# RWKV-7 recurrence: turn by feature and affine step one period later, keys' start before the block inversion, tile loads in two parts

## The reference, cut to what matters

```python
kk = heads(k * k_k); kk = kk * rsqrt(max(sum(kk * kk), 1e-24))
k = k * (1.0 + (a - 1.0) * k_a)
decay = exp(-exp(w))
# per token, 16 heads of 64 x 64:
sk = state @ kk_t
state = state * w_t - sk (x) (kk_t * a_t) + v_t (x) k_t
y = state @ r_t
# then per head:
y = (y - mean) * rsqrt(var + GN_EPS) * ln_w + ln_b
bonus = sum(r * k * r_k) * v
y = (y + bonus) * g
```

## Time and profile before

| | |
|---|---|
| time, three executions | 3096.55, 3098.84, 3102.23 us; median 3098.84 |
| the profiled execution's own time | 3100.76 us |
| its span | 3098.8 us |
| busy over the span | PE 2688.0 us (87%), DVE 1655.4 (53%), POOL 1257.8 (41%), ACT 932.7 (30%) |
| recurrence | about 1626 to 2235 us |
| mean granted TensorE clock | 0.944 of full speed |

### The profile page before, as it was taken

One profiled execution on the slowest core, in us unless ns is written; L12 is line 12 of the kernel. 1 busy time (PEld: TensorE's weight loads), 2 busy tenths in 40 slices (PEclk: granted clock), 3 DMA queues, 4 the chain that ended last, 5 costly groups with the idle time before them and its releaser, 6 DMA issues. The chain is left out here.

```text
span 3098.8 us, 48344 instructions
## 1 busy us (share of the span) xinstructions
PE 2688.0 (87%) x20064; PEld 2195.1 (71%) x20064; DVE 1655.4 (53%) x2070; ACT 932.7 (30%) x1543; POOL 1257.8 (41%) x630
## 2 busy tenths in 40 slices
PE   1787898999999999899994777777569999999999
PEld 1565666888877788677773667666557888878887
DVE  6844545756536444669734666776314544434444
ACT  2434433222233222455542223222124222222221
POOL 2532244444454444443433234333136344444443
PEclk9889998999999999999996888888789999999999
DMA  6421233555523223375563333333243233323333
GB/s 233 165 73 35 89 121 113 170 168 170 170 84 106 89 88 103 95 171 154 144 157 89 90 84 86 81 88 76 47 112 89 95 95 95 102 89 95 102 96 122
DMA packets 313433, 343.31 MB, mean 111 GB/s; under 512 B 231041, under 2 KB 231169, under 8 KB 313217
## 3 DMA queue, kind: packets, MB, share of 16 engines
q1 hardware_dynamic: 313216, 340.23, 37.5%
HBM read 298.29 MB, written 40.89 MB: 109 GB/s over the span
## 5 line engine op out<-in xcount | busy, mean ns | idle before, releaser
L687 POOL TENSOR_TENSOR wl<-w,wh 128x1024 fp32r<-128x1024 f32 x368 | 907.4, 2472 | 1304.0 <-ACT wh L728 1303.9
L180 PE MATMUL ps<-hi,wh 128*128 128x512 f32 x2208 | 881.8, 399 | 56.6 <-POOL wl L687 42.9
L181 PE MATMUL ps<-lo,wh 128*128 128x512 f32 x2208 | 868.3, 393 | 0.0
L182 PE MATMUL ps<-hi,wl 128*128 128x512 f32 x2208 | 867.9, 393 | 0.0
L728 ACT ACTIVATE wh<-w 128x1024 fp32r<-128x1024 f32 x368 | 388.1, 1056 | 716.2 <-DMA w<-in_ffn_w_in 528.7
L180 PEld LDWEIGHTS ps<-hi,wh 128*128 128x128 f32 x2208 | 419.8, 190 | 159.5 <-POOL wl L687 43.1
L994 DVE SCALAR_TENSOR_TENSOR xt<-ps,mod,xt 128x512 f32<-128x512 f32 x384 | 286.5, 750 | 431.8 <-PE ps L182 431.5
L181 PEld LDWEIGHTS ps<-lo,wh 128*128 128x128 f32 x2208 | 419.8, 190 | 89.3 <-issue 3.5
L182 PEld LDWEIGHTS ps<-hi,wl 128*128 128x128 f32 x2208 | 419.3, 190 | 89.6
L999 DVE TENSOR_TENSOR act<-ps,silu 128x512 f32<-128x512 f32 x88 | 60.9, 692 | 456.3 <-PE ps L182 456.3
L180 PE MATMUL ps<-act_hi,wh 128*128 128x512 f32 x704 | 281.7, 400 | 17.3 <-DVE act_lo L1003 9.7
(11 more groups left out here) (219 smaller groups left out, 3403.9 us busy)
## 6 DMA issues: line engine op xcount, KB each, us to landing
w<-in_ffn_w_in SPq DMA_DIRECT2D x176, 512.0 KB, 3.7
piece<-in_ada_w SPq DMA_DIRECT2D x96, 512.0 KB, 4.7
w<-in_ffn_w_out SPq DMA_DIRECT2D x88, 512.0 KB, 3.7
w<-in_w_rkv SPq DMA_DIRECT2D x48, 512.0 KB, 4.1
scratch<-silu SPq DMA_DIRECT2D x48, 256.0 KB, 3.1
scratch<-act SPq DMA_DIRECT2D x48, 256.0 KB, 3.0
w<-in_wqk SPq DMA_DIRECT2D x20, 512.0 KB, 4.7
xt<-in_xT SPq DMA_DIRECT2D x4, 2048.0 KB, 10.3
```

The lines of the kernel that those rows point to most:

```text
L180: pe.matmul(out, w_hi(k), x_hi(k), start=first and k == 0, stop=False)
L181: pe.matmul(out, w_hi(k), x_lo(k), start=False, stop=False)
L182: ins = pe.matmul(out, w_lo(k), x_hi(k), start=False, stop=last and k == kc - 1)
L687: pool.tensor_tensor(wl[n % NW][:, :, :], wr[n % NW][:, :, :], wh[n % NW][:, :, :].bitcast(F32), ALU.subtract).then_inc(*wlo.up)
```

## The change

A sixth argument, zp = chunk c-2, is added to `period`, and c runs to 17. `by_feature` (PE), `affine` (DVE), `finish` (POOL) and `store_z` (SP) are called for zp, one period later, and earlier in the lists. `begin(w)` moves ahead of `invert`, `bonus_value` ahead of `scale`. PE's `norms` waits for the bonus value. ACT's `squares` goes ahead of the copy of the turned keys. The tile loads are split: k, a and the decay's sigmoid as soon as POOL has k2, lprev and b of the chunk before; r behind `blocks_out`. POOL's `keys` does lprev first, bias has two buffers, and in POOL's list `bonus_and_bias` comes first.

```diff
-    for c in range(-RING, NC + 1):
-        period(at(c + 3), at(c + 2), at(c + 1), at(c), at(c - 1))
+    for c in range(-RING, NC + 2):
+        period(at(c + 3), at(c + 2), at(c + 1), at(c), at(c - 1), at(c - 2))
 # SP
 def load_tiles(ch):
-    sp.wait_ge(*g["rk_done"].at(ch))
-    sp.wait_ge(*g["ar_done"].at(2 * ch))
+    sp.wait_ge(*g["k2_done"].at(ch))
+    sp.wait_ge(*g["lq_done"].at(ch))
+    sp.wait_ge(*g["b_done"].at(ch))
     settle(sp)
-    for n, x in ((0, rt), (1, kt_), (3, st_), (4, at_)):
+    for n, x in ((1, kt_), (4, at_), (3, st_)):
         sp.dma_start(x[:, :, :], scr[n, ...]).then_inc(*g["tiles_in"].up)
+def load_r(ch):
+    sp.wait_ge(*g["rk_done"].at(ch))
+    sp.wait_ge(*g["ar_done"].at(2 * ch))
+    settle(sp)
+    sp.dma_start(rt[:, :, :], scr[0, ...]).then_inc(*g["r_in"].up)
-def period(w, x, d, y, zz):
-    load_gate(y); blocks_out(x); load_tiles(w); blocks_in(x); blocks_back(d); load_values(w); store_z(zz)
+def period(w, x, d, y, zz, zp):
+    load_gate(zz); load_tiles(w); blocks_out(x); load_r(w); blocks_in(x); store_z(zp); blocks_back(d); load_values(w)
 # POOL
 def keys(ch):
+    pool.wait_ge(*g["l_done"].at(ch + 1))
+    pool.tensor_tensor(lprev[:, :, :], lcum[:, :, :], st_[:, :, :], ALU.subtract).then_inc(*g["lq_done"].up)
     pool.wait_ge(*g["t1_done"].at(ch + 1))
...
-    pool.wait_ge(*g["l_done"].at(ch + 1))
-    pool.tensor_tensor(lprev[:, :, :], lcum[:, :, :], st_[:, :, :], ALU.subtract).then_inc(*g["lq_done"].up)
 def bonus_terms(ch):
     pool.wait_ge(*g["k2_done"].at(ch + 1))
+    pool.wait_ge(*g["r_in"].at(ch + 1))
-    normed_keys(x), bonus_and_bias(zz), bonus_terms(x), finish(zz), keys(w)
+    bonus_and_bias(zz), normed_keys(x), bonus_terms(x), finish(zp), keys(w)
 # ACT
-    root(zz), token_out(x, 1), squares(w)
+    root(zz), squares(w), token_out(x, 1)
 # PE
 def norms(ch):
     pe.wait_ge(*g["sq_done_w"].at(ch + 1))
-    pe.wait_ge(*g["z1_done"].at(max(ch - 3, 0)))
+    pe.wait_ge(*g["bonus_done"].at(ch))
 def by_feature(ch):
     pe.wait_ge(*g["ybd_done"].at(ch + 1))
     pe.wait_ge(*g["bonus_done"].at(min(ch + 4, NC)))
+    pe.wait_ge(*g["mx_done"].at(min(ch + 5, NC)))
-    solve_x(zz), level_x(y, 0), level_t(y, 0), solve_u(zz), level_x(y, 1), outputs(zz), gram(x, 0), state_products(zz),
-    level_t(y, 1), by_token(x, 0), by_token(x, 1), bonus_sums(x), gram(x, 1), by_feature(zz), by_token(x, 2), norms(w)
+    solve_x(zz), by_feature(zp), level_x(y, 0), level_t(y, 0), solve_u(zz), level_x(y, 1), outputs(zz), gram(x, 0),
+    state_products(zz), level_t(y, 1), by_token(x, 0), by_token(x, 1), bonus_sums(x), gram(x, 1), by_token(x, 2), norms(w)
 # DVE
 def begin(ch):
-    dve.wait_ge(*g["tiles_in"].at(4 * ch + 4))
+    dve.wait_ge(*g["tiles_in"].at(3 * ch + 3))
     dve.wait_ge(*g["kb_done"].at(ch))
+    dve.wait_ge(*g["rk_done"].at(ch))
 def decayed(ch):
...
+    dve.wait_ge(*g["r_in"].at(ch + 1))
-    bounded(x), level(y, 0, ..), products_k(d), level(y, 1, ..), decayed(x), centre(zz), products_b(x), new_state(zz), decayed_keys(x),
-    invert(d), variance(zz), invert_last(d), scale(zz), bonus_value(x), begin(w), affine(zz), decay_sums(w)
+    bounded(x), affine(zp), level(y, 0, ..), products_k(d), level(y, 1, ..), decayed(x), centre(zz), products_b(x), new_state(zz),
+    decayed_keys(x), begin(w), invert(d), variance(zz), invert_last(d), bonus_value(x), scale(zz), decay_sums(w)
```

More of the change, by code:

```diff
@@ L94 @@
 wkv_ybd_done wkv_yf_done wkv_z1_done wkv_bias_done wkv_z_step wkv_zeros g_in0*16 g_in1*16
-wkv_chunk_used wkv_post_done wkv_sub_step wkv_sub_done n_out*16 nd_in*16 t_out*16 img_zero*16 t_in0*16 t_in1*16 z_stored*16 z_in0*16 z_in1*16 z_hi z_lo stored*16
+wkv_chunk_used wkv_post_done wkv_r_in*16 wkv_sub_step wkv_sub_done n_out*16 nd_in*16 t_out*16 img_zero*16 t_in0*16 t_in1*16 z_stored*16 z_in0*16 z_in1*16 z_hi z_lo stored*16
 w_in0*16 w_in1*16 w_in2*16 w_in3*16 whi wlo tile_done x_done silu_done act_mul act_hi act_done
@@ L1248, in wkv_phase @@
                 state, xst, ust = st("state"), st("x_st"), st("u_st")
-                yc, ysq, yn, z, bias = st("y_centred"), st("y_sq"), st("y_norm"), st("z"), st("bias")
+                yc, ysq, yn, z, bias = st("y_centred"), st("y_sq"), st("y_norm"), st("z"), [st(f"bias{b}") for b in range(2)]
                 mean, var = sb("mean", [P, PAIRS], c=c), sb("var", [P, PAIRS], c=c)
@@ L1258, in wkv_phase @@
                          "m_step yc_done ysq_done var_done yrt_done yrn_done ybd_done yf_done z1_done bias_done z_step "
-                         "zeros sub_step sub_done chunk_used post_done").split()
-                g = {n: sig("wkv_" + n, 16 if n in ("tiles_in", "v_in") else 1) for n in names}
+                         "zeros sub_step sub_done chunk_used post_done r_in").split()
+                g = {n: sig("wkv_" + n, 16 if n in ("tiles_in", "v_in", "r_in") else 1) for n in names}
                 g_in = [sig(f"g_in{b}", 16) for b in range(2)]
@@ L1321, in load_tiles @@
                         def load_tiles(ch):
+                            sp.wait_ge(*g["k2_done"].at(ch))
[3 more added lines that the diff above has]
+                            for n, x in ((1, kt_), (4, at_), (3, st_)):
+                                sp.dma_start(x[:, :, :], scr[n, bass.ds(ch, 1)].rearrange("c p a n -> (c p) a n")).then_inc(*g["tiles_in"].up)
+                        def load_r(ch):
                             sp.wait_ge(*g["rk_done"].at(ch))
@@ L1325, in load_tiles @@
                             settle(sp)
-                            for n, x in ((0, rt), (1, kt_), (3, st_), (4, at_)):
-                                sp.dma_start(x[:, :, :], scr[n, bass.ds(ch, 1)].rearrange("c p a n -> (c p) a n")).then_inc(*g["tiles_in"].up)
+                            sp.dma_start(rt[:, :, :], scr[0, bass.ds(ch, 1)].rearrange("c p a n -> (c p) a n")).then_inc(*g["r_in"].up)
                         def load_values(ch):
@@ L1375, in _ @@
                                     sp.dma_start(image(t_img[b, w], h), state[h * HEAD:(h + 1) * HEAD, :, :]).then_inc(*img_zero.up)
-                        def period(w, x, d, y, zz):
-                            if y is not None:
-                                load_gate(y)
+                        def period(w, x, d, y, zz, zp):
+                            if zz is not None:
+                                load_gate(zz)
+                            if w is not None:
+                                load_tiles(w)
                             if x is not None:
@@ L1382, in period @@
                             if w is not None:
-                                load_tiles(w)
+                                load_r(w)
                             if x is not None:
                                 blocks_in(x)
+                            if zp is not None:
+                                store_z(zp)
                             if d is not None:
@@ L1389, in period @@
                                 load_values(w)
-                            if zz is not None:
-                                store_z(zz)
                         periods(period)
@@ L1422, in bonus_and_bias @@
                             pool.wait_ge(*g["bonus_done"].at(ch + 1))
-                            pool.tensor_tensor(bias[:, :, :], bonus[ch % RING][:, :, :], column(V_LNB), ALU.add).then_inc(*g["bias_done"].up)
+                            pool.tensor_tensor(bias[ch % 2][:, :, :], bonus[ch % RING][:, :, :], column(V_LNB), ALU.add).then_inc(*g["bias_done"].up)
                         def finish(ch):
@@ L1427, in finish @@
                             pool.wait_ge(*g["bias_done"].at(ch + 1))
-                            pool.tensor_tensor(z[:, :, :], z[:, :, :], bias[:, :, :], ALU.add).then_inc(*g["z_step"].up)
+                            pool.tensor_tensor(z[:, :, :], z[:, :, :], bias[ch % 2][:, :, :], ALU.add).then_inc(*g["z_step"].up)
                             pool.wait_ge(*g["z_step"].at(ch + 1))
@@ L1431, in finish, with period @@
                             pool.tensor_tensor(z[:, :, :], z[:, :, :], gt[ch % 2][:, :, :], ALU.mult).then_inc(*g["post_done"].up)
-                        def period(w, x, d, y, zz):
-                            if x is not None:
-                                normed_keys(x)
+                        def period(w, x, d, y, zz, zp):
                             if zz is not None:
@@ L1438, in period @@
                             if x is not None:
-                                bonus_terms(x)
-                            if zz is not None:
-                                finish(zz)
+                                normed_keys(x), bonus_terms(x)
+                            if zp is not None:
+                                finish(zp)
                             if w is not None:
@@ L1527, in period @@
                                 root(zz)
+                            if w is not None:
+                                squares(w)
                             if x is not None:
```

(15 more changed lines are left out.)

## The result

| | before | after |
|---|---|---|
| time, median of 7 runs each | 3100.12 us | 3108.72 us (3103.58 to 3112.06) |
| ratio, 95% interval | | 1.0025 (1.0015 to 1.0034) |
| the profiled execution's own time, span | 3100.76, 3098.8 | 3104.75, 3102.8 |

The change made the kernel slower by 0.25%, 8.6 us in the medians. Forecast were 3096 us and, as the likeliest, no change that can be told. The time lies inside the whole range of 3082 to 3113 us, but above the forecast's own range of 3089 to 3103, and the change is clear of the noise in the direction to which 27 in 100 were given.

What follows compares the result with a forecast made beforehand. No engine is full; a chain through several engines, 0.9 us longer than a DRAM round trip, sets the period. Steady +0.7, head -1.2, drain -2.7 sum to -3.2 us: 3096 us from 3098.84; own range 3089 to 3103, whole 3082 to 3113.

Steps and rivals of the forecast that it cites:

- Part 1: Turn by feature and affine step one period later: the DRAM round trip then sets the first level product, -0.9 us a period.
- T to X: From T, DVE's copy of the inverted diagonal blocks, to X, PE's next first level product: 10.1 us a period.
- Part 2: Keys' start (kk and k) in DVE's run ahead of the inversion: +1.3 us a period; its loads in time, 0.
- X to T: DVE's long run from PE's first level product (X) to its copy of the inverted blocks (T): 24.05 us a period.
- Part 3: POOL through before DVE's two decayed-key steps, which save 1.8 us; gram product then held by the outputs: -1.5 us.
- Part 4: SP's reordered waits, stores and tile loads, and the doubled bias: 0 us.
- Part 5: PE's new idle stretch ahead of the first level product lowers its clock, giving 24.05 us from X to T.
- Rival B: Clock lost for most of X to the outputs: period 35.7 us, 3114 us in all, slower; chance 0.22.
- steady sum: Twelve steady periods of the recurrence: 34.15 us a period against 34.09, +0.7 us over the twelve.
- Head: First passes of the recurrence: -5.1 us from earlier loads and key steps, +3.9 in the next three periods, -1.2 us.
- Drain: End of the recurrence: last chunk's right side starts ahead of the turn by feature, -2.7 us.
- Outside the recurrence: Time before and after the recurrence: no term in the sum, so no change.

Runs made afterwards that it cites:

- e_back_late: As e_begin_back, with POOL's two last steps of z also waiting for b_dec: 3073.57 us, ratio 0.9917 to the kernel before.
- e_pe_fill: Changed kernel plus five unread constant products on PE between the turn by feature and the first level's products: 3090.74 us, ratio 0.997 to the kernel before.
- e_begin_back: Changed kernel with the keys' start (two DVE steps) moved back behind the bonus value: 3077.57 us, ratio 0.9928 to the kernel before.

## Why the prediction was wrong

Its mechanism was right, and its sum was too low, on the wrong side of nothing. Point by point, with the means of the profiles of either kernel:

- *Part 1, X set by the DRAM round trip.* Right: the norms' product at T + 1.11, X 0.09 us behind the landing in every period. The size was off. The prediction took 10.1 us for T to X; it was 10.3, 10.5 and 10.4 in the three profiles, 0.3 more. The landing itself came at T + 10.2 to 10.4, where the two profiles of before give 10.2 and 9.9, and the 0.09 us from landing to start was left out.
- *Part 2, the keys' start, +1.3.* Right: X to T is 22.84 us with it (the clock up, POOL out of the way) and 21.5 without it, in e_back_late.
- *Part 3, POOL's order, -1.5.* Right: the two steps took 1.50 and 1.53 us in the mean before and 0.75 and 0.68 after, 0.78 and 0.75 in the second profile:

```profile
L1713 DVE TENSOR_TENSOR ar<-r,e_pos 128x512 f32<-128x512 f32 x12 | 9.0, 752 | 3.7 <-ACT e_neg L1471 3.7
L1716 DVE SCALAR_TENSOR_TENSOR ar<-kk,e_prev 128x512 f32<-128x512 f32 x12 | 8.2, 684 | 0.0
```

- *Part 4, SP and the loads, 0.* Right: in the period shown k's load is issued at T + 10.5, and DVE comes to kk at T + 26.6 (1982.47) without a wait.
- *Part 5, the clock.* It fell as the row of before had shown. Of 33 periods (eleven in each profile after) six were at 1.00 behind X, with 22.8 to 23.5 us from X to T; 21 had 2.8 to 3.4 us at 0.50 and took 23.8 to 24.4; six had 5.1 to 5.9 us and took 24.9 to 25.2. The mean is 24.2 against the 24.05 taken (and 24.05 over all twelve, since the last one has no keys' start). That it fits so well is in part luck, for the one row of before stood for three kinds of period. Rival B took 2.6 us over the 23.0 with the clock up; six periods of 33 came near that, with 2.0 to 2.4 over 22.84.
- *The steady sum* was therefore wrong in size: +0.7 us forecast, 413.5 against 409.0 measured, +4.5. The term that makes the difference is T to X: 10.4 + 24.05 = 34.45 a period, where the forecast had 10.1 + 24.05 = 34.15. Most of the 0.3 us is the last load, which took 4.2 us to land where it took 3.9 before, within a spread of 3.2 to 5.3; why it was slower is not shown.
- *Head, -1.2.* Wrong: +0.6 in the mean. The first T is 2.7 to 3.4 us earlier against the first load, where 3.8 was estimated, but then the third pass takes it back: X to T is 25.0 and 25.1 us in two profiles, with over 5 us at 0.50, and 23.9 in the third, against 22.75 + 1.3.
- *Drain, -2.7.* From the last X to the last store it is -2.4 in the mean (34.3 against 36.7); but the period before it is 1.1 longer (29.7 against 28.6, where the two profiles of before give 29.9 and 27.3), of which I have not traced the cause. -1.4 in all.
- *Outside the recurrence* 0 was taken, by leaving it out of the sum, and 3.3 us were found. About two thirds of that are the 6 us ahead of the recurrence in one profile, a third the 4 us behind it in another, and of those the rows show 1.6 as the clock's.

The step that failed is the sum, and in it first the term T to X: 10.1 us were taken for the round trip and 10.4 measured, 3.8 us over twelve periods, more than the whole forecast change of 3.2. The others were the head (-1.2 taken, +0.6 found), the drain (-2.7 taken, -1.4 found) and what lies outside, which had no term (3.3 found). The prediction had allowed 4 us of doubt for the round trip and as much for head and drain, but gains and losses of 11 to 18 us each nearly cancelled in its sum, so that errors of that size decided the sign, and all four were to the same side.

The Trainium skill, "TensorE: Matmul & The Clock Gate", section "HAM oscillation", describes a loop in which a wait of 3 to 5 us for a DMA in each tile makes every tile start at the lower clock. The waits ahead of X were 1.7 to 4.7 us here, and the trace agrees in 27 of 33 periods; falls came behind waits of 1.8 us, too, well under the page's 3.

What the falls add up to is shown by e_pe_fill: with the idle stretch filled the changed kernel takes 17 us less, of which its steady periods show 12, and the change turns from a loss of 0.25% into a gain of 0.3%.

## What to carry to other kernels

Before work is taken from a chain, look what else ends at its end: here a transfer with only 0.9 us of slack stood beside 11 us of engine work, so the 4 us taken out bought 0.6 and an idle PE. Work that such a transfer hides is free where it is, and costs its full length where it is moved in front of the transfer; moving it back, taking POOL's two steps out of DVE's way, and waiting for each half of the transfer only where it is used, together made the kernel 1.5% faster than before. Idle time put ahead of a dependent run of small products has a second price, which comes in the products behind it. And where a sum is a small difference of large terms, an error of 0.3 us in a term that comes twelve times is enough to turn its sign.

## What the runs showed of the hardware

- DVE's step with two SBUF operands took 0.69 us alone and 1.5 to 1.58 beside POOL's steps.
- Idle stretches of PE ahead of X brought a fall of the clock in 27 of 33 periods of the changed kernel (2.9 to 3.2 us in the mean of its three profiles), in none of twelve in e_begin_back (1.6 us) and in five of twelve in e_back_late (1.9 us). The length of a single stretch does not decide: 1.81 us were followed by a fall and 3.00 by none in one and the same profile, 2.75 by none in e_begin_back. The loss is 1.0 to 2.4 us of a run of 23.
- The same idle stretch of 2.13 us ahead of the kernel's last group of products was followed by a fall in four of ten profiles, which cost 1.6 us, and by none in six. What decides between them is not shown here.
- The time of code that was not touched, 864 us behind the last store, took one of two values 3.5 us apart.
- Five products a period that nobody reads, 2.4 us of PE time that was idle anyway, made the kernel 17 us faster.
